# A decoder trunk with a feature-major residual: output projection, FFN opening and final sum

## The reference, cut to what matters

```python
def rms_norm(x, g):
    y = x * rsqrt(mean(x * x, axis=-1) + EPS)
    return y * g

m = merged @ w_out                                    # 2048 -> 2048
x = x + rms_norm(m, norm_mix_post)                    # called x1 below
g, v = split(rms_norm(x, norm_ffn_pre) @ w_ffn_up)    # 2048 -> 2 x 5632
f = (silu(g) * v) @ w_ffn_down                        # 5632 -> 2048
return x + rms_norm(f, norm_ffn_post)
```

## Time and profile before

| | |
|---|---|
| median of 3 runs | 2395.49 us |
| profiled execution, its own time | 2396.26 us |
| its span in the profile | 2394.5 us |
| mean granted clock of TensorE | 0.997 |
| TensorE busy | 2380.6 us, 99% of the span |
| VectorE busy | 1662.2 us, 69% |
| ScalarE busy | 1075.3 us, 45% |
| mean DMA traffic | 187 GB/s |

### The profile page before, as it was taken

How to read it: one execution, slowest core, us unless ns; L and a number is a source line. 1 busy time by engine, 2 the same in 40 slices (tenths; PEclk the granted TensorE clock), 3 DMA queues, 4 the chain that set the end, 5 groups by cost and what they waited for, 6 DMA issues and landing times.

```text
span 2394.5 us, 50036 instructions
## 1 busy us (share of the span) xinstructions
PE 2380.6 (99%) x19326; PEld 2330.7 (97%) x19326; DVE 1662.2 (69%) x3010; ACT 1075.3 (45%) x1599; POOL 59.4 (2%) x118
## 2 busy tenths in 40 slices
PE   9999999999999999999999999999999999999998
PEld 9999999999999999999999999999999999999998
DVE  7898988979888877798966654655555555544444
ACT  6553544535455445545643334543333333433332
POOL 1000000000000002100400000000000000000000
PEclk9999999999999999999999999999999999999999
DMA  7676766667576678555877666565555556555443
GB/s 211 198 215 196 229 186 202 208 194 240 179 215 193 206 249 213 147 158 164 239 204 208 197 195 194 153 172 166 161 164 168 164 159 174 165 193 171 159 158 121
DMA packets 556327, 448.34 MB, mean 187 GB/s; under 512 B 30544, under 2 KB 534960, under 8 KB 555056
## 3 DMA queue, kind: packets, MB, share of 16 engines
q1 hardware_dynamic: 544896, 429.02, 59.5%
q0 software_dynamic: 5376, 7.11, 1.4%
q10 hardware_dynamic: 5904, 10.15, 1.2%
HBM read 409.39 MB, written 36.76 MB: 186 GB/s over the span
## 4 chain that ended last, share of the span: by engine, by line
PE 97%; DVE 1%; issue 0%; DMA 0%; ACT 0%; SPq 0%; DVEq 0%; ACTq 0%
PE acc L1994 30%; PE acc L1995 30%; PE acc L1996 30%; PE side L1981 2%; PE side L2080 1%; PE side L2151 1%; PE side L2132 1%; PE side L2268 0%; PE side L2309 0%; PE side L2291 0%; DMA xnat<-in_x_prompt_dram 0%; PE side L2119 0%; PE side L2112 0%; PE side L2116 0%; PE side L2137 0%
## 5 line engine op out<-in xcount | busy, mean ns | idle before, releaser
L1248 DVE TENSOR_TENSOR w_lo<-raw,w_hi 128x1024 fp32r<-128x1024 f32 (+2 forms) x692 | 830.3, 1208 | 513.9 <-ACT w_hi L765 509.4
L765 ACT ACTIVATE w_hi<-raw 128x1024 fp32r<-128x1024 f32 (+2 forms) x692 | 716.6, 1045 | 913.7 <-PE acc L1996 901.3
L1994 PE MATMUL acc<-h_hi,w_hi 128*128 128x288 f32 x3472 | 1031.6, 297 | 0.0
L1996 PE MATMUL acc<-h_hi,w_lo 128*128 128x288 f32 x3472 | 1024.4, 295 | 0.0
L1995 PE MATMUL acc<-h_lo,w_hi 128*128 128x288 f32 x3472 | 1024.3, 295 | 0.0
L1994 PEld LDWEIGHTS acc<-h_hi,w_hi 128*128 128x128 f32 x3472 | 651.7, 188 | 7.3 <-issue 2.5
L1995 PEld LDWEIGHTS acc<-h_lo,w_hi 128*128 128x128 f32 x3472 | 652.2, 188 | 1.4
L1996 PEld LDWEIGHTS acc<-h_hi,w_lo 128*128 128x128 f32 x3472 | 651.9, 188 | 0.0
L1994 PE MATMUL acc<-f_hi,w_hi 128*128 128x288 f32 x704 | 208.1, 296 | 0.0
L1996 PE MATMUL acc<-f_hi,w_lo 128*128 128x288 f32 x704 | 207.8, 295 | 0.0
L1995 PE MATMUL acc<-f_lo,w_hi 128*128 128x288 f32 x704 | 207.6, 295 | 0.0
(11 more groups left out here) (358 smaller groups left out, 2533.0 us busy)
## 6 DMA issues: line engine op xcount, KB each, us to landing
raw<-in_w_in_dram SPq DMA_DIRECT2D x512, 256.0 KB, 3.5
raw<-in_w_ffn_up_dram SPq DMA_DIRECT2D x352, 256.0 KB, 3.5
raw<-in_w_ffn_down_dram SPq DMA_DIRECT2D x160, 256.0 KB, 2.9
raw<-in_w_ssm_out_dram SPq DMA_DIRECT2D x128, 256.0 KB, 3.5
raw<-in_w_glu_dram SPq DMA_DIRECT2D x128, 256.0 KB, 3.7
h<-in_state_ssm_dram SPq DMA_DIRECT2D x32, 512.0 KB, 6.7
out_ssm_sample_dram<-h SPq DMA_DIRECT2D x32, 512.0 KB, 3.0
raw<-in_w_out_dram SPq DMA_DIRECT2D x64, 256.0 KB, 3.2
```

Of the source, the lines that this page charges most:

```text
L765: copy = lambda out, in_, **k: nc.scalar.activation(out, in_, ACT.Copy, **k)
L1248: tt(w_lo[:, slot, 0:n], raw[:, slot, 0:n], w_hi[:, slot, 0:n].bitcast(F32), ALU.subtract).then_inc(lo_ready, 1)
L1994: mm(o_, wh, xh[:, kt, :], start=first and i == 0, stop=False)
L1996: done = mm(o_, wl, xh[:, kt, :], start=False, stop=last and i == n - 1)
```

## The change

The residual is kept feature-major throughout, so nothing is turned: `m_turn`, `f_turn`, `x1_turns` and `rows_copy` are gone. The host hands x in a second, feature-major layout (`x_features`), takes one feature-major output `y`, and turns it itself.

m stays in `mW` (16 tiles of 128x288). After `proj(7)`, whose last chunk is `closing` (its first block is finished first, and the sums of `sst` stand inside it), the factor is spread by TensorE to bank `s0`. Tile by tile VectorE scales and adds (`x1_scale`, `x1_add`), ScalarE rounds, VectorE takes the remainder.

The FFN opens by K tile: the first 16 chunks hold one K tile each by 4 blocks of gate and 4 of linear columns, into all eight PSUM banks, so that chunk u needs only tile u. ScalarE then copies the four pairs out to `fo` (`opening_copy`). Each turn of the opening's loop has, on ScalarE, the split of chunk u+3, the rounding of tile u+4, the square of tile u; on VectorE the split of chunk u+3, the scale of tile u+4, the remainder of tile u+3, the add of tile u+4 and the sum of square u. `up` goes on from group 4.

SyncE stores x1 straight to the output `y`, between the weights of chunk 15 and chunk 16. At the end VectorE multiplies f by the factor in eight pieces of 128x576, and POOL adds each to `y` in DRAM with an accumulating transfer.

In `up`, `down`, `proj` the waits and calls for the turns are gone; `summed` writes its tile into `mW` or `fW`; `down(7)` ends with `closing` as well.

```diff
--- before.py
+++ after.py
...
-    mT, at = sb("mT", [P, 3, D_MODEL], F32, used["ya"][0])
-    mt, at = sb("mt", [P, 2, 2, T], F32, at)
-    msq, at = sb("msq", [P, 3, T], F32, at)
+    mW, at = sb("mW", [P, KT, T], F32, used["ya"][0])
+    msq, at = sb("msq", [P, 2, T], F32, at)
+    fo, at = sb("fo", [P, 4, 3, T], F32, at)
     assert at <= used["mg_hi"][0]
-    x1T, at = sb("x1T", [P, 3, D_MODEL], F32, used["v_hi"][0])
-    ss2, at = sb("ss2", [P, 3, 4], F32, at)
...
-        turn_bank = [*side, acc[0], acc[1]]
+        opening_bank = [(acc[2], acc[3]), (acc[0], acc[1]), (side[0], side[1]), (side[2], side[3])]
...
+            sp.dma_start(x1F[:, :, :], a['x_features']).then_inc(sem("xT_landed"), 16)
...
-            up_chunks(0)
-            up_chunks(1)
-            sp.wait_ge(*reach("x1_ready", 12))
-            for c, (t0, n) in enumerate(TOK):
-                sp.dma_start(x1_dram[t0:t0 + n, :], x1T[0:n, c, :]).then_inc(sem("x1_stored"), 16)
-            with sp.Fori(2, FT) as k:
+            def opening_load(u):
+
+                sp.wait_ge(lo_ready, C_UP + u - (RING - 1))
+                src = w_up[u * P:(u + 1) * P, :].rearrange("p (s n) -> p s n", s=2)[:, :, 0:4 * P]
+                for k in range(2):
+                    sp.dma_start(raw[:, u % 4, k * 512:(k + 1) * 512], src[:, k, :]).then_inc(landed[u % 4], 16)
+
+            for u in range(KT):
+                opening_load(u)
+            sp.wait_ge(*reach("x1_ready", KT))
+            sp.dma_start(o['y'], x1F[:, :, :]).then_inc(sem("x1_stored"), 16)
+            with sp.Fori(4, FT) as k:
...
+            pool.wait_ge(sem("x1_stored"), 16)
+            for j in range(8):
+                pool.wait_ge(sem("y_ready"), j + 1)
+                pool.dma_start(o['y'][:, 2 * j:2 * j + 2, :], fW[:, 2 * j:2 * j + 2, :], accum_op=ALU.add).then_inc(sem("y_added"), 16)
...
+            def rstd_copy(n):
+
+                act.wait_ge(*reach("rstd_spread", n))
+                act.wait_ge(*reach("x1_scaled", 1))
+                copy(rstd[:, :], s0[:, 0:T]).then_inc(sem("rstd_copied"), 1)
...
+            def h2_round(i):
+                act.wait_ge(*reach("x1_ready", i + 1))
+                copy(h_hi[:, i, :], x1F[:, i, :], scale=vec[:, N_FPRE + i:N_FPRE + i + 1]).then_inc(sem("h2_rounded"), 1)
+            def x1_square(i):
+                wait(act, "x1_summed", i - 1)
+                nc.scalar.activation(msq[:, i % 2, :], x1F[:, i, :], ACT.Square).then_inc(sem("x1_squares"), 1)
+            def opening_split(u):
+                split(C_UP + u, (C_UP + u) // 4, u % 4)
+            def opening_copy(b):
+                if b < 3:
+                    act.wait_ge(*reach("opening_blocks", b + 1))
+                else:
+                    act.wait_ge(multiplied, C_UP + KT)
+                copy(fo[:, b, 1, :], opening_bank[b][0][:, 0:T])
+                copy(fo[:, b, 2, :], opening_bank[b][1][:, 0:T]).then_inc(sem("opening_copied"), 1)
+            def f_tanh(k, v):
+                act.wait_ge(*reach("f_scaled", k + 1))
+                nc.scalar.activation(v[:, 0, :], v[:, 1, :], ACT.Tanh, scale=0.5).then_inc(sem("f_tanh"), 1)
+            def f_round(k, v):
+                act.wait_ge(*reach("f_out", k + 1))
+                copy(f_hi[:, ds(k, 1), :].rearrange("p o t -> p (o t)"), v[:, 2, :]).then_inc(sem("f_rounded"), 1)
+            for i in range(4):
+                h2_round(i)
+            for u in range(KT):
+                opening_split(u + LEAD)
+                if u + 4 < KT:
+                    h2_round(u + 4)
+                x1_square(u)
+            opening_copy(0)
+            opening_copy(1)
+            opening_split(19)
+            opening_copy(2)
+            opening_copy(3)
+            rms_tokens(2, 0)
+            opening_split(20)
+            rstd_copy(2)
+            opening_split(21)
+            f_tanh(0, fo[:, 0])
+            f_tanh(1, fo[:, 1])
+            opening_split(22)
+            f_tanh(2, fo[:, 2])
+            f_round(0, fo[:, 0])
+            f_tanh(3, fo[:, 3])
+            f_round(1, fo[:, 1])
+            f_round(2, fo[:, 2])
+            f_round(3, fo[:, 3])
 
...
+            def x1_scale(i):
+                if i < 2:
+                    dve.wait_ge(*reach(("rstd_spread", "rstd_copied")[i], 1))
+                by = s0[:, 0:T] if i == 0 else rstd[:, :]
+                tt(mW[:, i, :], mW[:, i, :], by, ALU.mult).then_inc(sem("x1_scaled"), 1)
+            def x1_add(i):
+                dve.wait_ge(*reach("x1_scaled", i + 1))
+                tt(x1F[:, i, :], mW[:, i, :], x1F[:, i, :], ALU.add).then_inc(sem("x1_ready"), 1)
+            def h2_remainder(i):
+                dve.wait_ge(*reach("h2_rounded", i + 1))
+                stt(h_lo[:, i, :], x1F[:, i, :], vec[:, N_FPRE + i:N_FPRE + i + 1], h_hi[:, i, :].bitcast(F32),
+                    ALU.mult, ALU.subtract).then_inc(sem("h2_ready"), 1)
+            def square_add(i):
+                dve.wait_ge(*reach("x1_squares", i + 1))
+                tt(sst[:, :], sst[:, :], msq[:, i % 2, :], ALU.add).then_inc(sem("x1_summed"), 1)
...
+            x1_scale(0)
+            x1_add(0)
+            for i in range(3):
+                x1_scale(i + 1)
+                h2_remainder(i)
+                x1_add(i + 1)
+            dve.wait_ge(sem("sst_zero"), 2)
+            for u in range(KT):
+                opening_split(u + LEAD)
+                if u + 4 < KT:
+                    x1_scale(u + 4)
+                if u + 3 < KT:
+                    h2_remainder(u + 3)
+                if u + 4 < KT:
+                    x1_add(u + 4)
+                square_add(u)
+                if u + 1 < KT:
+                    dve.wait_ge(*reach("x1_summed", u + 1))
+            opening_split(19)
+            rstd_tokens(2)
+            opening_split(20)
+            dve.wait_ge(*reach("rstd_copied", 2))
+            dve.wait_ge(*reach("opening_copied", 4))
+            f_scale(0, fo[:, 0, 1, :], fo[:, 0, 2, :], fo[:, 0])
+            f_scale(1, fo[:, 1, 1, :], fo[:, 1, 2, :], fo[:, 1])
+            opening_split(21)
+            f_scale(2, fo[:, 2, 1, :], fo[:, 2, 2, :], fo[:, 2])
+            f_scale(3, fo[:, 3, 1, :], fo[:, 3, 2, :], fo[:, 3])
+            f_silu(0, fo[:, 0])
+            opening_split(22)
+            f_remainder(0, fo[:, 0])
+            f_silu(1, fo[:, 1])
+            f_silu(2, fo[:, 2])
+            f_remainder(1, fo[:, 1])
+            f_silu(3, fo[:, 3])
+            f_remainder(2, fo[:, 2])
+            f_remainder(3, fo[:, 3])
...
-            dve.wait_ge(*reach("rstd_tokens", 3))
-            dve.wait_ge(*reach("x1_landed", 16 * 6))
-            for j in range(4):
-                dve.wait_ge(*reach("fT_copied", 2 * j + 2))
-                cols = slice(j * 512, (j + 1) * 512)
-                if j == 3:
-                    v = fT[:, 2, 0:512]
-                    stt(v, v, sx2[:, 4:5], xr2[:, :], ALU.mult, ALU.add).then_inc(sem("y_ready"), 1)
-                for c, x in enumerate((xr0, xr1)):
-                    v = fT[:, c, cols]
-                    stt(v, v, sx2[:, 2 + c:3 + c], x[:, cols], ALU.mult, ALU.add).then_inc(sem("y_ready"), 1)
+            dve.wait_ge(*reach("rstd_spread", 3))
+            for j in range(8):
+                v = fW[:, 2 * j:2 * j + 2, :]
+                tt(v, v, bc(s0[:, 0:T], 2, 1), ALU.mult).then_inc(sem("y_ready"), 1)
...
+                        if m == 1 and i == 0:
+                            pe.wait_ge(*reach(s_sum, 14))
+                            token_sums(sst, start=True, stop=False)
...
+            rstd_spread(1)
+            pe.wait_ge(freed, 23)
+            hold(HOLD)
+            def opening_chunk(u):
+                pe.wait_ge(lo_ready, C_UP + u + 1)
+                pe.wait_ge(*reach("h2_ready", u + 1))
+                for b in range(4):
+                    if u == 0 and b == 1:
+                        pe.wait_ge(freed, 24)
+                    if u == 0 and b == 2:
+                        pe.wait_ge(*reach("x1_scaled", 1))
+                        pe.wait_ge(*reach("rstd_copied", 1))
+                    for m in range(2):
+                        o_ = opening_bank[b][m][:, 0:T]
+                        at_ = m * 4 * P + b * P
+                        wh, wl = w_hi[:, u % 4, at_:at_ + P], w_lo[:, u % 4, at_:at_ + P]
+                        mm(o_, wh, h_hi[:, u, :], start=u == 0, stop=False)
+                        mm(o_, wh, h_lo[:, u, :], start=False, stop=False)
+                        done = mm(o_, wl, h_hi[:, u, :], start=False, stop=u == KT - 1)
+                    if u == KT - 1 and b < 3:
+                        done.then_inc(sem("opening_blocks"), 1)
+                done.then_inc(multiplied, 1)
+            def x1_sums():
+                pe.wait_ge(*reach("x1_summed", KT))
+                pe.wait_ge(*reach("opening_copied", 4))
+                token_sums(sst, start=True, stop=True).then_inc(sem("sums_ready"), 1)
+                if isinstance(k, int) and k < 6:
```

(51 more changed lines are left out.)

280 lines of the change are left out of this document (71 added, 209 removed).

## The result

The changed kernel takes 2414.45 us, the median of 6 runs (2413.11 to 2415.82). The kernel before, beside it, took 2395.61 us (2395.3 to 2396.18). The ratio is 1.0078, with a 95% interval of 1.0067 to 1.0089: slower by 18.8 us. I had forecast 2403.1 us in a range of 2388 to 2410. The sign was right, and the time lies outside the range.

A forecast was written before the change was run, and what follows sets the result against it. The prediction took TensorE to bound the kernel, busy 2380.6 of 2394.5 us. Its terms, -4.6 + 0.7 + 11.4 + 1.5 - 4.6 + 0.7 + 2.5, summed to +7.6 us, giving 2403.1 us in a range of 2388 to 2410.

The forecast's parts named there:

- Turns go, sums of squares: Output and down projections: removed turns save 4.6 us in each; sums of squares inside the last chunk add 0.7 each.
- L: Start of the last projection matmul, 1521.69 in the kernel before; times at the FFN's start are counted from it.
- Start of the FFN: First FFN matmul, set by nine holding matmuls of 3.3 us: at L+6.6, 3.6 earlier than before.
- Does the opening keep that pace?: Opening's feeding loop: no, 4.2 us a turn against TensorE's 3.19, so 7.6 us lost by chunk 15.
- rival A: Opening's feeding loop: it keeps TensorE's pace and all stalls go, 2384.7 us; chance 0.15.
- The store of x1 ahead of the next weights: Ahead of chunk 16: weights land 9.5 us after the store's issue, and TensorE stalls 9.3 us.
- rival B: Ahead of chunk 16: the loop stalls but weights overtake the store, landing after 4.6 us; 2397.5 us; chance 0.15.
- Clock: Chunk 16: the idle 9 us ahead of it lowers the granted clock, costing +1.5 us (0 to 2).
- The tail: After the last down matmul: products end at 9.6, last accumulating transfer takes 5.9; 15.5 us, +2.5.
- Rival C: Kernel's end: accumulating transfers run at half of 323 GB/s, tail 20.8 us, total 2408.4 us; chance 0.12.
- the seam: From L to the first down matmul, between output projection and FFN: forecast +12.9 us.

The follow-up runs named there:

- e1: Changed kernel, but in each opening turn VectorE does scale, remainder and add of x1 ahead of its split: 2393.31 us, ratio 0.9988.
- e2: Changed kernel, but SyncE stores x1 after the weights of groups 4 and 5, not ahead of chunk 16: 2402.93 us, ratio 1.0028.
- e4: Changed kernel, but POOL's last eight transfers overwrite y without accumulating, leaving out the residual's addition: 2406.44 us in one run.
- e10: e3 with four accumulating transfers of 576 KB at the end in place of eight: 2392.05 us in one run.
- e9: e3, but x1 is read back to SBUF, VectorE and POOL (three of eight pieces) add it, SyncE stores plainly: 2386.02 us, ratio 0.9959.
- e3: Changed kernel with x1's work ahead of VectorE's split and the x1 store after groups 4 and 5: 2392.32 us, ratio 0.9985.
- e5: Changed kernel, but SyncE stores f over x1 with plain transfers, leaving out the residual's addition: 2404.67 us in one run.

## Why the prediction went wrong, by its steps

- **Turns go, sums of squares.** Right: -3.7 and -3.9 measured where -3.9 was foreseen for each. The first is known to about 1 us only, by the scatter of L.
- **Start of the FFN.** Right: L+6.79 for L+6.6, set by the holding matmuls, which took 3.69 with a granted clock of 0.59 from 1521.4 to 1525.1.
- **"Does the opening keep that pace?"** The mechanism was right and e1 shows it; rival A falls. The size was short. I had 4.2 us a turn and L+8.7 for its first split; measured are 4.34 and L+9.5 (1527.52). The turn's extra comes from the remainder's pace (0.43, for which I used the 0.38 of another operation), from the rounding's (0.44 for 0.385), and from the hand-over to VectorE (1.14 after the split's start for 1.09). One turn of the twelve took 4.7, and why is open. Chunk 15 ended at L+68.3 for L+65.2: the loop cost 10.5 us, not 7.6.
- **"The store of x1 ahead of the next weights."** Right within 1 us: landing 10.3 for 9.5, hole 8.8 for 9.3, ended by the copy that stands behind three splits, as worked out. e2 shows it, and rival B falls.
- **Clock.** 2.5 (5.66 less 3.19) for 1.5. I scaled the cost from a stretch with 0.63; after the hole the clock was 0.50 for nearly the whole chunk. That the short gaps would cost the clock nothing was right: it was 1.00 from 1552 to 1588.
- **The tail: the step that failed.** The products ended 9.7 us after the last down matmul, for 9.6 foreseen. That agreement is luck: they began at 4.3 and not at 3.3, because the spread took 1.78 and not 0.8, and then took 5.4 where 6.3 was left for them. "POOL issues in 0.56 each, so it keeps up" held: the issues start 0.61 us apart. But "I take 5.9, nearer the 144 KB row" for the last accumulating transfer should have been 12.6. That is 6.7 of the 10.4 us by which the sum was short.

  The choice had no reason behind it: my own line through the two rows gave 8.6 (8.4 for 288 KB in the unit of the rows), and I went under it. But the line would have fallen short too, with a tail of 18.2. The rows for 72 and 144 KB were small plain transfers, the 72 KB ones issued every 0.56 us (some 130 GB/s, below both rates), and I treated the eight as separate, so that only the last one's landing counted. In fact they share a rate: 2.36 MB at about 205 GB/s take 11.5 us, and more with the slower first slices, where VectorE delivers them in 5.4 us, so a backlog builds from the first piece. e4 shows that the accumulation does it, e10 that it goes by bytes.

  Rival C had this mechanism, with a tail of 20.8 us; measured is 22.3. Its 16.6 us from first issue to end came true to the tenth, partly by luck: it took 162 GB/s where 205 flowed, and left out the slow first slices. The 1.5 that it lacks is the first issue, at 5.7 and not at 4.2. I gave C 0.12 because no row spoke for it, though the price of an operation that the trace doesn't show needed a bound by rate as well as by latency. My upper bound of +5.2 for the tail was below the +9.2 that came.

The two errors, 3.4 in the seam and 6.7 in the tail, went the same way; with rival C's tail and the rest as it was, the forecast would have been its 2408.4; with the seam as measured too, 2411.8. Of the 2.6 that are left, 1.5 is the real tail over C's and 1.0 is that the profiled execution lay 0.2 below its median, where the one of before lay 0.8 above.

## What to carry to other kernels

When two engines feed a third and hand work to each other in each turn, add up the turn along the hand-overs, not each engine's load: the same instructions took 4.34 or 2.80 us depending on which stood first. Put a large store behind the loads that the next stage needs, or among them only when chunks are in hand. Before an accumulating transfer replaces an add at the end of a kernel, price it by bytes over its own rate from the first piece to the last; here an add on VectorE and POOL with plain stores was 6.3 us faster (e9 against e3).

## What the runs showed of the hardware that was not expected

- Accumulating transfers to DRAM moved at 200 to 211 GB/s in steady flow, plain ones from the same queue at some 350, from SyncE's at 378 to 406 (e5). POOL's issues of 288 KB took 1.0 to 2.9 us with accumulation, overlapping, and 0.54 to 0.59 without; of 576 KB with accumulation 0.9. The Trainium skill ("DMA: Bandwidth & Descriptors", Anatomy of one DMA) gives a fit for a plain transfer of POOL's queue, 2.0 us + bytes/436e3, an estimate of 2.7 us for 288 KB; measured is 3.6 plain and 8.6 accumulating, in a series of eight.
- Nine short holding matmuls, five or none made no difference that the whole time can tell. In the stretch that they touch, nine are 1.2 us better than none, and five in one execution 1.2 better than nine.
- A store of 2.36 MB held up the 512 KB of weights queued behind it until 10.3 us after its issue, with TensorE waiting (changed kernel) and without (e1).
